# Seven of eleven pairs of the down projection as seven block products each, with part of the splitting done by accumulating DMAs

## What is computed

```
ffn = (silu(h @ w_ffn_gate) * (h @ w_ffn_up)) @ w_ffn_down    # 512x1024 -> 512x2816 -> 512x1024
h   = layer_norm(DEEPNORM_ALPHA * h + ffn, ln2_g, ln2_b)       # everything float32
```

## Time and profile before

| | us |
|---|---|
| median of 3 runs (734.34 to 735.02) | 734.7 |
| the profiled execution's own time | 735.12 |
| its span in the profile | 733.4 |

### The profile page before, as it was taken

One profiled execution on the slowest core, in us unless ns is written; L12 is line 12 of the kernel. 1 busy time (PEld: TensorE's weight loads), 2 busy tenths in 40 slices (PEclk: granted clock), 3 DMA queues, 4 the chain that ended last, 5 costly groups with the idle time before them and its releaser, 6 DMA issues.

```text
span 733.4 us, 11797 instructions
## 1 busy us (share of the span) xinstructions
PE 720.4 (98%) x4347; PEld 639.9 (87%) x4347; DVE 510.8 (70%) x912; ACT 331.5 (45%) x537; POOL 151.1 (21%) x164
## 2 busy tenths in 40 slices
PE   9999999999999999999999999999999999999995
PEld 7889887888888987888889899999999998888884
DVE  2424287797788885675798678998898886233576
ACT  3413377467777776522435144444444443313500
POOL 2608081513334431000000212222222210000000
PEclk9999999999999999999999999999999999999998
DMA  8524324202111203633641122333233324232202
GB/s 250 175 89 122 109 60 144 78 8 71 45 59 59 58 1 107 238 106 130 223 116 58 57 87 87 114 114 108 70 108 114 114 106 150 89 114 88 83 30 86
DMA packets 57459, 73.82 MB, mean 101 GB/s; under 512 B 3888, under 2 KB 44368, under 8 KB 57296
## 3 DMA queue, kind: packets, MB, share of 16 engines
q1 hardware_dynamic: 57280, 72.32, 30.6%
q0 software_dynamic: 144, 1.05, 0.7%
HBM read 70.21 MB, written 2.10 MB: 99 GB/s over the span
## 4 chain that ended last, share of the span: by engine, by line
PE 92%; DVE 4%; ACT 2%; issue 1%; DVEq 0%; POOL 0%; ACTq 0%; POOLq 0%
PE ps L1617 82%; PE ps L1629 5%; PE ps L1625 2%; PE ps L1626 2%; ACT prob L869 1%; DVE prob L1276 1%; DVE ptl L1063 1%; ACT wh L681 1%; DVE wl L1063 0%; DVE wl L1053 0%; DVE prob L1230 0%; PE ps L1780 0%; PE ps L1781 0%; DVE rinv L1227 0%; DVE rinv L1226 0%
## 5 line engine op out<-in xcount | busy, mean ns | idle before, releaser
L1617 PE MATMUL ps<-wh,xh 128*128 128x512 f32 (+1 forms) x376 | 145.0, 386 | 0.1
L1617 PE MATMUL ps<-wh,xl 128*128 128x512 f32 (+1 forms) x376 | 143.4, 382 | 0.0
L1617 PE MATMUL ps<-wl,xh 128*128 128x512 f32 (+1 forms) x376 | 143.3, 381 | 0.0
L1617 PE MATMUL ps<-xh,wh 128*128 128x256 f32 (+1 forms) x416 | 135.2, 325 | 1.1 <-DVE wl L1053 1.1
L1617 PE MATMUL ps<-xh,wl 128*128 128x256 f32 (+1 forms) x416 | 131.8, 317 | 0.0
L1617 PE MATMUL ps<-xl,wh 128*128 128x256 f32 (+1 forms) x416 | 131.6, 316 | 0.0
L1053 DVE TENSOR_TENSOR wl<-stage,wh 128x2048 fp32r<-128x2048 f32 (+1 forms) x29 | 66.0, 2277 | 93.7 <-ACT wh L687 64.5
L1617 PE MATMUL ps<-ath,wh 128*128 128x256 f32 (+1 forms) x280 | 86.0, 307 | 0.0
L1617 PE MATMUL ps<-ath,wl 128*128 128x256 f32 (+1 forms) x280 | 86.0, 307 | 0.0
L1617 PE MATMUL ps<-atl,wh 128*128 128x256 f32 (+1 forms) x280 | 86.0, 307 | 0.0
L1617 PEld LDWEIGHTS ps<-xh,wl 128*128 128x128 f32 x416 | 79.3, 191 | 5.4
(11 more groups left out here) (285 smaller groups left out, 1351.3 us busy)
## 6 DMA issues: line engine op xcount, KB each, us to landing
stage<-in_w_in SPq DMA_DIRECT2D x28, 512.0 KB, 4.5
stage<-in_w_ffn_gate SPq DMA_DIRECT2D x22, 512.0 KB, 4.7
stage<-in_w_ffn_up SPq DMA_DIRECT2D x22, 512.0 KB, 4.4
stage<-in_w_ffn_down SPq DMA_DIRECT2D x22, 512.0 KB, 3.8
stage<-in_w_out SPq DMA_DIRECT2D x8, 512.0 KB, 4.7
arena<-in_x SPq DMA_DIRECT2D x8, 256.0 KB, 6.0
stage<-in_w_in SPq DMA_DIRECT2D x8, 256.0 KB, 6.3
stage<-in_w_branch_nsa SPq DMA_DIRECT2D x4, 512.0 KB, 7.0
```

The lines of the kernel that those rows point to most:

```text
L1617: return pe.matmul(out, (sh, sh, sl)[i], (mh, ml, mh)[i], start=start and i == 0, stop=stop and i == 2)
```

## The change

The matrix product of a pair is seen as a 2 x 2 block product: two halves of the tokens (256 each), the two hidden tiles, two halves of the 1024 columns. Strassen's way takes seven block products in place of eight and needs sums of blocks. Seven pairs are done so, in two passes over them: pass one takes three of the seven products for each pair (units 0 to 6, weights 128x1536 with no sums), pass two the other four (units 7 to 13, weights loaded again, 128x2048, three of the four weight blocks replaced by sums). Unit 14 is a plain pair, and the last three units, 15 to 17, are plain pairs taken token tile by token tile as before. There are now three staging buffers (`mix` is the third).

- The sums of activations are 256 wide adds on DVE (`first_sums`, `second_sum`, `fourth_sum`) with splits of their results.
- Of the three weight sums of a unit of pass two, DVE makes two and a half: a first addition is an accumulating DMA of 128x512 inside the staging buffer, then DVE does three adds of 512 (`third_and_second`, `fourth`). ACT splits after all of them.
- The product banks are saved by ACT (`keep`) or added into `y` by DVE in 22 adds (`evict`) while PE does unit 14, since each product goes to several blocks of the result.
- For units 15, 16 and 17 the low parts are made as at L657: ACT negates and copies, POOL issues one accumulating DMA of 128x2048, waits for it, counts it, and goes to the next.

The diff, cut to its core (`...` where lines are left out):

```diff
-    N_DOWN = FT // 2
+    N_PAIR = FT // 2 - 4
+    N_DOWN = 2 * N_PAIR + 4
...
+            for t in range(N_DOWN):
+                sp.wait_ge(w_lo, U_DOWN + (t - 2 if t >= 3 else min(t, 1) - 1))
+                st, j = down_stage(t), pair_of(t)
...
+            for t in range(N_PAIR, 2 * N_PAIR):
+                st = down_stage(t)
+                pool.wait_ge(d_arrived[t % 3], down_count(t))
+                pool.dma_start(st[:, 0:512], st[:, 512:1024], accum_op=ALU.add).then_inc(e1_in[t % 3], 16)
+
+            for i, t in enumerate(range(N_DOWN - 3, N_DOWN)):
+                pool.wait_ge(neg_ok, i + 1)
+                pool.dma_start(down_w(wl, t), down_stage(t), accum_op=ALU.add).then_inc(low_in, 16)
+                pool.wait_ge(low_in, 16 * (i + 1))
+                pool.wait_ge(w_hi, U_DOWN + t + 1)
+                pool.wait_ge(w_lo, U_DOWN + t)
+                pool.memset(scrap[:, :], 0.0).then_inc(w_lo, 1)
...
+            def w_hi_of(t):
+
+                act.wait_ge(w_used, U_DOWN + t - 1)
+                if N_PAIR <= t < 2 * N_PAIR:
+                    act.wait_ge(e_ok, 3 * (t - N_PAIR + 1))
+                act.wait_ge(d_arrived[t % 3], down_count(t))
+                hi(down_w(wh, t), down_stage(t)[:, 0:down_width(t)]).then_inc(w_hi, 1)
+
+            def w_both_of(t):
+
+                if t != N_DOWN - 2:
+                    act.wait_ge(w_used, U_DOWN + 2 * N_PAIR + (1 if t == N_DOWN - 1 else 0))
+                act.wait_ge(d_arrived[t % 3], down_count(t))
+                act.mul(down_w(wl, t), down_stage(t), -1.0).then_inc(neg_ok, 1)
+                hi(down_w(wh, t), down_stage(t)).then_inc(w_hi, 1)
...
+            w_both_of(N_DOWN - 3)
+            a_hi_of(N_DOWN - 2)
+            w_both_of(N_DOWN - 2)
+            a_hi_of(N_DOWN - 1)
+            w_both_of(N_DOWN - 1)
...
+            def third_and_second(t):
+
+                dve.wait_ge(e1_in[t % 3], 16 * ((t - N_PAIR) // 3 + 1))
+                dve.tensor_tensor(quarter(t, 1), quarter(t, 1), quarter(t, 3), ALU.add).then_inc(e_ok, 1)
+                dve.wait_ge(e_ok, 3 * (t - N_PAIR) + 1)
+                dve.tensor_tensor(quarter(t, 3), quarter(t, 0), quarter(t, 3), ALU.add).then_inc(e_ok, 1)
...
+            for p in range(2 * N_PAIR):
+                t = p + 1
+                a_lo_of(t)
+                if t < N_PAIR:
+                    if p:
+                        h1_lo_of(p - 1)
+                    second_sum(t)
+                    fourth_sum(t)
+                else:
+                    if p - 1 < N_PAIR:
+                        h1_lo_of(p - 1)
+                betas = N_PAIR <= t + 1 < 2 * N_PAIR
+                if betas and t >= N_PAIR:
+                    third_and_second(t + 1)
+                w_lo_of(t)
+                if t < N_PAIR:
+                    h4_lo_of(t)
+                if betas:
+                    if t < N_PAIR:
+                        third_and_second(t + 1)
+                    fourth(t + 1)
+                if p == 0:
+                    fact_of(n, 0)
+                    fact_of(n, 1)
...
+            t = 2 * N_PAIR
+            pe.wait_ge(w_lo, U_DOWN + t + 1)
+            pe.wait_ge(a_lo, t + 1)
             for m in range(MT):
+                if m == 0:
+                    pe.wait_ge(kept, 4)
+                else:
+                    pe.wait_ge(evicted, (4, 8, 10)[m - 1])
+                for f in range(2):
+                    for half in range(2):
+                        last = down(t, m, half, f, f == 0, False)
             last.then_inc(w_used, 1)
...
                 for half, j in order:
+                    t = N_DOWN - 3 + j
                     if m == 0 and half == 0:
+                        pe.wait_ge(w_lo, U_DOWN + t + 1)
+                        pe.wait_ge(a_lo, t + 1)
```

More of the change, by code:

```diff
@@ new lines, in w_both_of, with keep @@
+            def w_both_of(t):
[4 more added lines that the diff above has]
+                hi(down_w(wh, t), down_stage(t)).then_inc(w_hi, 1)
+            def keep(to, banks):
+                for i, bank in enumerate(banks):
+                    last = act.copy(to[:, i, :], ps[:, bank, :])
+                last.then_inc(kept, 1)
@@ L1027, in _ @@
[L1027 to L1039, removed]
@@ new lines, in evict @@
+            def evict(m, half, bank, op, start=False):
+                ym = y[:, m, 512 * half:512 * half + 512]
+                if start:
+                    dve.scalar_tensor_tensor(out=ym, in0=ym, scalar=ALPHA, in1=bank, op0=ALU.mult,
+                                             op1=op).then_inc(evicted, 1)
+                else:
+                    dve.tensor_tensor(ym, ym, bank, op).then_inc(evicted, 1)
+            a_lo_of(N_DOWN - 3)
+            dve.wait_ge(q_done, 4)
+            for i in range(2):
+                evict(i, 1, ps[:, FIVE_BANKS[i], :], ALU.add, True)
+                evict(2 + i, 1, ps[:, FIVE_BANKS[i], :], ALU.add, True)
@@ L1604, in _, with add_last @@
+            dve.wait_ge(evicted, 18)
+            for i in range(2):
+                evict(2 + i, 1, q3_kept[:, i, :], ALU.subtract)
+            a_lo_of(N_DOWN - 1)
+            def add_last(m, half):
+                ym = y[:, m, 512 * half:512 * half + 512]
+                return dve.tensor_tensor(ym, ym, ps[:, ROW_BANKS[m][half], :], ALU.add)
+            dve.wait_ge(evicted, 22)
             for m in range(MT):
@@ L2019, in _ @@
                 seven(n)
[L2020 to L2033, removed]
@@ L2035, in _, with product_rows @@
[L2035 to L2040 removed]
+            def product_rows(banks, ah_, al_, q, t, start, stop, again=False):
+                c = slice(512 * q, 512 * q + 512)
+                for i, bank in enumerate(banks):
+                    tok = slice(P * i, P * i + P)
+                    last = mm3(ps[:, bank, :], ah_[:, tok], al_[:, tok], down_w(wh, t)[:, c], down_w(wl, t)[:, c],
+                               start, stop, again)
+                return last
@@ L2050, in _ @@
-            pe.wait_ge(w_lo, U_DOWN + 1)
-            pe.wait_ge(a_lo, 1)
-            for m in range(MT):
-                for half in range(2):
-                    last = down(m, half, 1, 0, w2d(wh, 0), w2d(wl, 0), False, False)
-            last.then_inc(w_used, 1)
-            down_unit(1, 1)
-            with pe.Fori(1, (N_DOWN - 3) // 2) as i:
-                for b in range(2):
-                    down_unit(2 * i + b, b)
-            late = ((0, w2d(wh, 0), w2d(wl, 0)),
-                    (2, late_h.rearrange("p (f n) -> p f n", f=2), late_l.rearrange("p (f n) -> p f n", f=2)),
-                    (3, w2d(wh, 1), w2d(wl, 1)))
+                last = product_rows(SEVEN_BANKS, *operand_of(t, 1), 1, t, begin, end)
@@ new lines, in _, with down @@
+                if end:
+                    last.then_inc(q_done, 1)
+                if begin:
+                    pe.wait_ge(kept, 3)
+                product_rows(FOUR_BANKS, *operand_of(t, 2), 2, t, begin, end).then_inc(w_used, 1)
+            def down(t, m, half, f, start, stop):
+                tok = slice(512 * f + P * m, 512 * f + P * m + P)
+                c = slice(1024 * f + 512 * half, 1024 * f + 512 * half + 512)
+                return mm3(ps[:, ROW_BANKS[m][half], :], down_a(xh, t)[:, tok], down_a(xl, t)[:, tok],
+                           down_w(wh, t)[:, c], down_w(wl, t)[:, c], start, stop)
```

290 lines of the change are left out of this document (213 added, 77 removed).

## The result

The changed kernel takes 760.9 us (median of 4 runs, 757.14 to 764.95) against 734.64: ratio 1.0358, 95% interval 1.0304 to 1.0412. It is slower, as forecast, but by 26 us where 15 were forecast, and it lies above the range of 741 to 758. Its executions differ by 8 us, those of the kernel before by 0.7. The profiled run took 760.38 us, its span is 758.6.

The account below looks back on a forecast made before the run. PE alone was taken to set the pace. -9.5 (fewer matmuls) + 3.0 (entry) + 7.2 (pass two) + 12.3 (tail) + 2.2 (clock) = +15.2 us on 735.12 gave 750.3, median 750; range 741 to 758.

Parts of the forecast that it names:

- the sums in the stage before: Activation sums on DVE in the gate and up stage, ahead of the down stage; the forecast left them out.
- the clock in pass two: PE's clock after waits in pass two; the forecast sum held no loss for it.
- pass two's waits: Three-buffer loop, 12.6 us per two units against PE's 10.9: unit 7 late 3.8, units 9 and 11 1.7 each, sum 7.2.
- The tail: Units 15 to 17: three accumulating DMAs of 8.7 us in sequence make units 16 and 17 late 6.1 each, sum 12.3.
- "-9.5" for 42 matmuls: Seven pairs on PE: 42 fewer matmuls at 0.2274 us each save 9.5 us, all on the path.
- The entry: Start of the down stage: PE waits for DVE 0.6 at the start, 1.6 at unit 1, 0.9 at unit 2, sum 3.0.
- The accumulating DMA of 128x512 ... I take 4.3: Small DMA in pass two's buffer loop: taken as 4.3 us, between ends of 3.2 and 5.0.
- The load in the same loop: Pass two's buffer loop: 0.2 to issue, 0.5 to the second DMA, 3.8 to its landing, together 4.5 us.
- sharing makes them slower: Rival: loads and accumulations run together in pass two, DMAs take 10 and 5.5 us, stalls 30, total 758; chance 0.10.
- The clock: Behind the last long tail wait, PE's matmuls run at 1.2 GHz: eleven slow ones taken, 2.2 us, between nothing and 4.8.
- DVE's work ... 5.0 us of 5.5, so it fits: Pass two, per unit: DVE's activation work 0.9, three adds 1.9 and 2.2 more make 5.0 us within PE's 5.5.
- DVE's own work 3.6: Pass one after the entry: DVE's work for a unit is 3.6 us, under PE's 4.1, so pass one holds.

Follow-up runs that it names:

- e7: Changed kernel with the two activation sums of a pair moved from the gate and up stage to pass one, before the third sum: 757.68 us, ratio 1.0304.
- e6: Changed kernel with the accumulating DMAs of units 16 and 17 replaced by DVE subtractions between its adds into y; unit 15 keeps its DMA: 748.89 us, ratio 1.0183.
- e8: Changed kernel with three edits: fourth add on DVE for the small DMA, tail splits on DVE, activation sums in pass one: 739.16 us, ratio 1.0064.
- e4: Kernel before the change, with probe accumulating DMAs on idle buffers added on POOL in the down stage, beside a load or after one: 734.14 us.
- e2: Changed kernel with the 128x512 accumulating DMA of each pass two unit replaced by the same addition on POOL: 753.24 us, ratio 1.0247.
- e3: Changed kernel with the three large tail DMAs replaced by one POOL subtraction each, ACT's negated copy dropped: 755.85 us, ratio 1.0286.
- e1: Changed kernel with the two sums of first_sums cut from 256 columns to 4, order and semaphores kept: 758.92 us.
- e10: e9 with DVE's sums woven, so that other instructions stand between sums that depend on one another; same instructions: 736.92 us, ratio 1.0033.
- e9: e8 with unit 7's split put ahead of unit 8's first three additions on DVE: 739.71 us, ratio 1.0068.

## Why the prediction was right in direction and short in size

The forecast sum is 10 us short. By size, these steps failed: the sums in the stage before, put at nothing, cost 4.85; the clock in pass two, put at nothing, cost 4.4; and pass two's waits, put at 7.2, came to 11.1, as the accumulating DMA and the load before it took longer than the rows that they were taken from. The tail was put 3.0 too high, which hid as much of the error.

- **"-9.5" for 42 matmuls**: the changed kernel's stage has 486 matmuls for 528, and PE keeps the old pace wherever it neither waits nor has a low clock. Nothing contradicts it, and no run tests it alone.
- **"The entry", 3.0**: right. Shifted by 4.85 us, the forecast starts of 605.9, 611.6 and 616.6 are 610.8, 616.5 and 621.5; measured 610.78, 616.33, 621.27. The terms given for unit 1 add up to 611.9 rather than 611.6, so the last tenths are luck.
- **Missing term: the sums in the stage before.** The prediction costs the change from the first down unit on, though `first_sums` stands in the loop before it. 4.85 us, shown by e7. The text on the kernel before itself says that this stage "lets it [DVE] end some microseconds behind PE": where DVE's order sets the pace of a loop, an added instruction costs its full length, and more.
- **"The accumulating DMA of 128x512 ... I take 4.3"**: mis-sized. The way of bounding it was sound for a quiet machine (ends 3.2 and 5.0, measured 3.3), but its only row ran alone. The profile page's median for five of the seven in the changed kernel is 4.7, and the two that matter at unit 7 took 7.2 and 6.6. The load in the same loop was priced by quiet rows too: from the split that frees the buffer (633.1) to POOL's issue it took 6.0 us for 4.5. With 1.5 more for the load and 2.3 for the DMA, and 0.2 less elsewhere, the loop took 16.2 us for 12.6, so unit 7 waited 7.3 us, not 3.8. The rival "sharing makes them slower" named this mechanism, with a chance of 0.10; it was worth far more, since the text itself counts 1.25 MB for each 5.5 us of pass two. That its 758 us lies near the result is luck: it takes 10 us for the large DMAs, which took 7.0 to 8.1, and has neither the stage before nor any price for the clock in pass two. Units 9 and 11 were to wait 1.7 each; unit 9 came in time, unit 11 waited 3.8.
- **"The clock"**: forecast for the tail alone. A wait of 7.3 us had the same price in pass two: unit 7's first twelve matmuls start 0.43 us apart, 2.7 us in all, and unit 11 lost 1.7. The forecast's own reading of the earlier trace rows, a clock that falls some 2 us after PE falls idle, called for it once the wait at 7 was put at 3.8, and the sum left it out. Behind the last tail wait it was 1.8 for 2.2.
- **"The tail", 12.3**: right in kind and too high, both waits released by POOL's memset. The DMAs took 7.8, 8.1 and 7.0 instead of 8.7, and the two waits, 5.0 and 1.9, with the slow matmuls between them came to 9.7. e6 took the tail's losses away and gained 12.0.
- **"DVE's work ... 5.0 us of 5.5, so it fits"**: right only while a DMA does one add. With that add DVE needs 5.75 a unit (e8), and in pass one 4.65 of PE's 4.1 once it has all sums. "DVE's own work 3.6" left out these sums and what a chain costs.

## What to carry to other kernels

Before costing a change, list every loop in which it puts an instruction, also those ahead of the stage that it is about, and ask of each which engine's order sets the pace there. Price a DMA by a row in which the same queues are as busy as they will be; where there is none, put a short one beside a load and measure, since a loop that is closed by a DMA multiplies the error by its passes. On an engine that is the bound, put an independent instruction between two that depend on one another: here that alone was worth 2.8 us, with not one instruction less.

## What the runs showed of the hardware that was not expected

- An accumulating DMA of 256 KB in SBUF took 3.3 us in quiet and 5.3 to 7.2 beside the load of 1 MB (e4); one of 1 MB 7.0 to 8.7 in quiet, and 9.6 and 10.3 beside a load.
- A POOL add or subtraction can hold up DVE instructions whose operands are all in SBUF (0.69 became 1.67 us in e2, 1.3 became 6.4 in e3); those of e3 that read PSUM kept their 0.6. POOL's DMA issues of 0.85 us did not slow the kernel before (e4, 734.14 beside 734.7).
- Two DVE instructions of 4 columns, put into a loop in a chain, cost 0.73 us of the 0.99 that two of 256 columns cost (e1).
- Of DVE's 256-column instructions, one that needs the one right before it starts 0.46 us after it, another 0.34 (e8, e10).
- A lower PE clock cost nothing where PE waits for another engine in every unit anyway: 13.00 and 13.01 us to unit 2 with it and without (e8, e9).
